# One kernel, one core: turning k and q by DVE blocks and DRAM, and scoring neighbouring tokens by one product sum per pair

## The reference, cut to what matters

```python
q = silu(q_raw)
log_f = logaddexp(log(lb), log1p(-lb) + log_sigmoid(f_raw))   # lb is 0 here: log_sigmoid(f_raw)
k = (1.0 - lb) * sigmoid(-f_raw)
...                                           # per chunk of 64 tokens, 8 heads of 128 channels
G = cumsum(g_t, axis=1)                       # g = log_f
att[t, s] = sum_c q[t, c] * k[s, c] * exp(G[t, c] - G[s, c])    # for s <= t
o_intra = att @ v
```

## Time and profile before

| | |
|---|---|
| time before, 3 runs | 2002.93 us (2002.09 to 2003.38) |
| the profiled execution, its own time | 2004.01 us |
| its span, first to last instruction | 2002.2 us |
| granted TensorE clock, mean | 0.999 |
| PE busy | 1988.7 us, 99% |
| DVE busy | 1723.3 us, 86% |
| ACT busy | 1212.6 us, 61% |
| PE on the chain that ended last | 91% |

### The profile page before, as it was taken

The page is one execution under the profiler, slowest core; times in us unless marked ns, Lnnn a source line. Parts: engine busy times, 40 slices in busy tenths (PEclk is TensorE's granted clock), DMA queues, the critical chain, the costliest instruction groups (busy, mean ns, idle before and its releaser), DMA issues.

```text
span 2002.2 us, 24409 instructions
## 1 busy us (share of the span) xinstructions
PE 1988.7 (99%) x9167; PEld 1647.1 (82%) x9167; DVE 1723.3 (86%) x1641; ACT 1212.6 (61%) x1216; POOL 170.9 (9%) x216
## 2 busy tenths in 40 slices
PE   9999999999999999999999999999999999999998
PEld 7888888888888888888888887888888888888886
DVE  5566776789999999999997467789999999999995
ACT  6755655555666656656657466565656666566664
POOL 0000000100111110111100000100111101111010
PEclk9999999999999999999999999999999999999999
DMA  8764443857898888988877644676988889988886
GB/s 283 253 213 165 157 147 133 280 197 237 267 265 254 248 258 253 268 253 258 246 238 227 194 144 147 218 235 226 268 262 253 248 248 271 262 261 246 252 238 185
DMA packets 237652, 463.50 MB, mean 231 GB/s; under 512 B 16561, under 2 KB 20945, under 8 KB 237457
## 3 DMA queue, kind: packets, MB, share of 16 engines
q1 hardware_dynamic: 203296, 389.08, 57.8%
q0 software_dynamic: 30496, 69.22, 16.5%
q10 hardware_dynamic: 3792, 4.34, 0.7%
HBM read 403.21 MB, written 17.29 MB: 210 GB/s over the span
## 4 chain that ended last, share of the span: by engine, by line
PE 91%; DVE 4%; DMA 2%; ACT 2%; issue 1%; SPq 0%; ACTq 0%; DVEq 0%
PE ps L1823 60%; PE ps L1623 28%; DMA raw<-in_w_ab_in 2%; PE ps L1714 1%; DVE w_lo L969 1%; DVE g_lo L1352 1%; DVE w_lo L1359 0%; PE ps L1981 0%; PE ps L1956 0%; ACT junk L544 0%; ACT w_hi L499 0%; PE ps L1969 0%; DVE w_sum L1340 0%; PE ps L1647 0%; DVE w_sum L1338 0%
## 5 line engine op out<-in xcount | busy, mean ns | idle before, releaser
L1352 DVE TENSOR_TENSOR g_lo<-g_raw,g_hi 128x2048 fp32r<-128x2048 f32 x240 | 545.7, 2287 | 6.5 <-ACT g_hi L768 0.5
L969 DVE TENSOR_TENSOR w_lo<-raw,w_hi 128x1024 fp32r<-128x1024 f32 x247 | 293.1, 1220 | 146.3 <-ACT w_hi L499 145.4
L759 ACT CAST g_hi<-g_raw 128x2048 fp32r<-128x2048 f32 x120 | 229.9, 1916 | 219.5 <-DVE g_raw L1326 215.8
L499 ACT ACTIVATE w_hi<-raw 128x1024 fp32r<-128x1024 f32 x247 | 253.2, 1055 | 146.3 <-DMA raw<-in_w_ab_in 56.5
L1623 PE MATMUL ps<-w_hi,xT_hi 128*128 128x512 f32 x672 | 264.2, 393 | 3.2 <-DVE w_lo L969 2.8
L1823 PE MATMUL ps<-g_hi,xT_hi 128*128 128x512 f32 x680 | 265.4, 390 | 0.1
L1823 PE MATMUL ps<-g_hi,xT_lo 128*128 128x512 f32 x680 | 264.6, 389 | 0.0
L768 ACT CAST g_hi<-g_raw 128x2048 fp32r<-128x2048 f32 x120 | 225.5, 1912 | 60.2 <-PE ps L1823 60.2
L1623 PE MATMUL ps<-w_hi,xT_lo 128*128 128x512 f32 x672 | 261.7, 389 | 0.0
L1623 PE MATMUL ps<-w_lo,xT_hi 128*128 128x512 f32 x672 | 261.5, 389 | 0.0
L1823 PE MATMUL ps<-g_hi,h0T_hi 128*128 128x512 f32 x640 | 249.2, 389 | 0.0
(11 more groups left out here) (232 smaller groups left out, 3134.2 us busy)
## 6 DMA issues: line engine op xcount, KB each, us to landing
g_raw<-in_w_ffn_in SPq DMA_DIRECT2D x320, 512.0 KB, 4.8
g_raw<-in_w_ffn_out SPq DMA_DIRECT2D x160, 512.0 KB, 4.8
raw<-in_w_ab_in SPq DMA_DIRECT2D x95, 512.0 KB, 4.9
x<-y POOLq DMA_DIRECT2D x80, 512.0 KB, 6.9
raw<-in_w_qkv SPq DMA_DIRECT2D x40, 512.0 KB, 4.6
raw<-in_w_ab_out SPq DMA_DIRECT2D x32, 512.0 KB, 4.7
raw<-in_w_ffn_in SPq DMA_DIRECT2D x32, 512.0 KB, 4.9
raw<-in_w_c_out SPq DMA_DIRECT2D x32, 512.0 KB, 5.0
```

Of the source, the lines that this page charges most:

```text
L499: act.activation(w_hi[:, s, :], raw[:, s % RAWS, :], ACT.Copy).then_inc(hi_ready, 1)
L759: act.copy(dst[:, 0:4, :].rearrange("p s w -> p (s w)"), src[:, :, :].rearrange("p s w -> p (s w)")).then_inc(group_hi_ready, 1)
L969: dve.tensor_tensor(w_lo[:, s, :], raw[:, s % RAWS, :], w_hi[:, s, :], ALU.subtract).then_inc(lo_ready, 1)
L1352: ins = dve.tensor_tensor(lo_part[:, 0:4, :].rearrange("p s w -> p (s w)"), src[:, :, :].rearrange("p s w -> p (s w)"), hi_part[:, 0:4, :] ...
```

## The change

PE's 32 transposes of k and q are gone, and so is the level for distance 1.

- k and q are turned like x: DVE turns blocks of 32 x 32 (`turn_kq`, L1162 of the changed kernel), POOL issues one DMA per token tile to DRAM and four back (`kq_dram` to `kq_rows`), and DVE copies the k rows to `kT`, ACT the q rows to `qT`, from SBUF instead of PSUM.
- The scores at distance 1 are one number per pair of tokens (2m, 2m+1) and head. POOL's DMAs gather the odd tokens of `lf` (`f_odd`) and of `q_tok` (`q_odd`) and the even ones of `kk` (`k_even`) into 128 rows. ACT takes the exponential of `f_odd`, DVE multiplies it by `k_even`, then by `q_odd`, sums over channels (`pair_sum`), two small DMAs bring the sums back to token rows, and DVE puts them into the scores through the same mask (`keep_pairs`).
- The other levels stay where they were, one per round from round 6 on.

```diff
+            def carry_out_kq(m):
+                pool.wait_ge(kq_turned, m + 1)
+                pool.dma_start(kq_dram[m % 2], kq_blk[m % 2][:, :, :, :].rearrange("p j h b -> p j (h b)")
+                               ).then_inc(kq_out[m % 2], 16)
+            def carry_in_kq(m):
+                i = m % 2
+                pool.wait_ge(kq_out[i], 16 * (m // 2 + 1))
+                if m >= 2:
+                    pool.wait_ge(kT_copied, i + 1)
+                for j in range(4):
...
+                    pool.dma_start(kq_rows[i][32 * j:32 * (j + 1), :, :, :].rearrange("p i h b -> p i (h b)"),
+                                   src).then_inc(kq_rows_in[i], 16)
...
+            gather(f_odd, lf, 1, f_odd_in)
+            pool.wait_ge(k_ready, 2)
+            gather(k_even, kk, 0, k_even_in)
+            carry_out_kq(0)
+            carry_out_kq(1)
+            carry_in_kq(0)
+            carry_in_kq(1)
+            pool.wait_ge(ab_read, 4)
+            pool.wait_ge(fk_ready, 1)
+            gather(q_odd, q_tok, 1, q_odd_in)
+            carry_out_kq(2)
+            carry_out_kq(3)
+            carry_in_kq(2)
+            carry_in_kq(3)
...
                 if r == 5:
                     ahead(5, 1)
                     for t in range(NT):
-                        act.wait_ge(item_done, 5 + t)
-                        act.copy(qT[:, t, :], side[t]).then_inc(side_free[t], 1)
+                        act.wait_ge(kq_rows_in[t], 128)
+                        act.copy(qT[:, t, :].rearrange("p (h i b) -> p h i b", h=HEADS, i=4),
+                                 kq_rows[t][:, :, :, :].rearrange("p i h b -> p h i b"))
...
+                if r == 3:
+                    act.wait_ge(f_odd_in, 32)
+                    act.activation(f_odd[:, :], f_odd[:, :], ACT.Exp).then_inc(f_odd_ready, 1)
                 if r - 1 == I_R:
+                    act.wait_ge(kq_turned, 2)
+                    act.wait_ge(pair_ready, 1)
...
                 if r == 4:
                     ahead(4, 0)
                     for t in range(NT):
-                        dve.wait_ge(item_done, 3 + t)
-                        dve.tensor_copy(kT[:, t, :], side[t]).then_inc(side_free[t], 1)
+                        dve.wait_ge(kq_rows_in[t], 64)
+                        dve.tensor_copy(kT[:, t, :].rearrange("p (h i b) -> p h i b", h=HEADS, i=4),
+                                        kq_rows[t][:, :, :, :].rearrange("p i h b -> p h i b")).then_inc(kT_copied, 1)
...
-            chunks(3, 0, 3, *X, PAIR[1])
-            for t in range(NT):
-                pe.wait_ge(k_ready, t + 1)
-                turn_tokens(2 + t, kk[:, t, :])
-            chunks(3, 3, 8, *X, PAIR[1])
+            chunks(3, 0, 8, *X, PAIR[1])
             pe.wait_ge(ab_read, 3)
-            chunks(4, 0, 4, *X, PAIR[0])
+            chunks(4, 0, 8, *X, PAIR[0])
             pe.wait_ge(ab_read, 4)
-            for t in range(NT):
-                turn_tokens(4 + t, q_tok[:, t, :])
...
```

More of the change, by code:

```diff
@@ L216, in trunk @@
         fnorm = sb("fnorm", [P, D], at=bias_at + 40 * KB)
+        k_even = sb("k_even", [P, 1024], at=at_mix + 4 * KB)
+        f_odd = sb("f_odd", [P, 1024], at=r1 + 16 * KB)
+        q_odd = sb("q_odd", [P, 1024], at=r1 + 16 * KB)
+        kq_blk = [sb(f"kq{i}_blk", [P, 4, HEADS, 32], at=r1 + (28 + 4 * i) * KB) for i in range(2)]
+        kq_rows = [sb(f"kq{i}_rows", [P, 4, HEADS, 32], at=r1 + (36 + 4 * i) * KB) for i in range(2)]
         x_blk = [sb(f"x{i}_blk", [P, 4, 4, NT, 32], at=r1 + (28 + 4 * i) * KB) for i in range(2)]
@@ L234, in trunk @@
         x_dram = [nc.dram_tensor(f"x{i}_dram", [P, 4, 8 * 32], F32, kind="Internal").ap() for i in range(2)]
+        kq_dram = [nc.dram_tensor(f"kq{i}_dram", [P, 4, 8 * 32], F32, kind="Internal").ap() for i in range(2)]
         ps = ctx.enter_context(nc.psum_tensor("ps", [P, 8, W], F32))
@@ L1112, in _ @@
                     dve.wait_ge(ab_read, 4)
+                    for t in range(NT):
+                        turn_kq(2 + t, q_tok)
                     eye = consts[:, C_IDENT:C_IDENT + 1, :].broadcast_to([P, HEADS, P])
+                    ahead(4, 7)
+                    dve.wait_ge(f_odd_ready, 1)
+                    dve.wait_ge(k_even_in, 32)
+                    dve.tensor_tensor(k_even[:, :], f_odd[:, :], k_even[:, :], ALU.mult).then_inc(fk_ready, 1)
                     for t in range(NT):
[L1115 to L1116 removed]
+                        if t:
+                            ahead(5, 0)
+                        after(dve.tensor_tensor(E[:, 0, :], q_tok[:, t, :], kk[:, t, :], ALU.mult))
+                        after(dve.tensor_reduce(o_sum[:, t, :], E[:, 0, :].rearrange("p (h d) -> p h d", h=HEADS), AX.X, ALU.add))
                         diag = o_sum[:, t, :].rearrange("p (h o) -> p h o", o=1).broadcast_to([P, HEADS, P])
@@ L1119, in _ @@
                     ins.then_inc(att_diag, 1)
+                if r == 3:
+                    dve.wait_ge(rel_out, 16)
+                    for t in range(NT):
+                        dve.wait_ge(k_ready, t + 1)
+                        turn_kq(t, kk)
                 if r == 2:
@@ L1691, in _ @@
             pe.wait_ge(ab_read, 2)
-            chunks(3, 0, 3, *X, PAIR[1])
-            for t in range(NT):
-                pe.wait_ge(k_ready, t + 1)
-                turn_tokens(2 + t, kk[:, t, :])
-            chunks(3, 3, 8, *X, PAIR[1])
+            chunks(3, 0, 8, *X, PAIR[1])
             pe.wait_ge(ab_read, 3)
-            chunks(4, 0, 4, *X, PAIR[0])
+            chunks(4, 0, 8, *X, PAIR[0])
             pe.wait_ge(ab_read, 4)
-            for t in range(NT):
-                turn_tokens(4 + t, q_tok[:, t, :])
[L1702 to L1715, removed]
+            chunks(5, 0, 8, *X, PAIR[1])
+            for r in range(6, 11):
+                pe.wait_ge(ab_read, r - 1)
+                chunks(r, 0, 8, *X, PAIR[r % 2])
+                for t in range(NT):
+                    pe.wait_ge(side_free[t], r - 5)
+                    pe.wait_ge(scaled, 2 * (r - 6) + t + 1)
+                    for h in range(HEADS):
+                        c = slice(h * P, (h + 1) * P)
+                        ins = pe.matmul(side[t][:, c], E[:, t, c], E[:, t, c], start=True, stop=True)
+                    ins.then_inc(item_done, 1)
             pe.wait_ge(ab_read, 10)
```

119 lines of the change are left out of this document (77 added, 42 removed).

## The result

The changed kernel takes 2014.43 us (median of 6 runs, 2013.57 to 2015.9) beside 2002.38 us of the kernel before on the same chip (6 runs, 2001.22 to 2003.38): 1.0057 times as long, 95% interval 1.0047 to 1.0067. It is slower by 12 us, where I had forecast 2002.3 and a range that ended at 2009.5.

A forecast was written before the change was run, and what follows sets the result against it. PE, busy 99% of the span, was taken to bound the kernel. Removing 8.3 us and adding 7.7 us of waits gave -0.6 us, forecast 2002.3 us on the scale of the median; the range ran from just below 1994.6 to 2009.5.

The forecast's parts named there:

- What goes: PE work and waiting removed: wait for G 1.34, turns of k 1.74 and q 1.67, first level 3.57; 8.3 us.
- the two places: New PE waits at (4,1), behind kT's copies, 2.0 us, and at (5,2), behind qT's copies, 5.7 us.
- 7.7 us of waiting in all: PE's total new waiting at (4,1) and (5,2) in the likeliest case, which had chance 0.40.
- The gathers of f_odd and k_even: Gathers starting around 75 us, claimed to cost nothing unless a landing takes over 8 us.
- The round trip of k: k's tiles ready at 87.6 and 88.8 us, 6.5 to first read, second copy to kT ends at 104.8.
- My bound for T, 109.2: Slow case for the second copy to kT, with landings of 8.9 and 8.1 us; PE waits 6.4 us.
- The turn of q: From second copy to kT until the lo of (5,2): 31.5 us, ready at 136.3, where PE wanted 128.6.
- idle DMA engines: During q's trip, DMA share 0.11 assumed: 5.0 us to first read, last landing 4.1 us.
- Rival 3, the clock: PE's granted clock falls during the wait at (5,2); chance 0.12.
- Rival 2, slow issues of POOL: POOL's issues in both turns take 1.02 instead of 0.553 us, 7.5 us more, 2009.8 us; chance 0.20.
- The rival's other condition: Both turns of k and q meeting landings near 8 us, with the same slower end as slow POOL issues.
- Hidden: Exponential of f_odd, 1 us, delays the hi of (3,6) within PE's some 3 us in hand, costing nothing.

The follow-up runs named there:

- experiment 5: Changed kernel with all three gathers and their waits out, the pair product reading other rows: 2003.42 us, ratio 0.9996 to the kernel before.
- experiment 9: Changed kernel with q's ways out ahead of the gather of q_odd on POOL and dynamic_dma_scratch_size 1792: 2007.81 us, ratio 1.0023.
- experiment 2: Changed kernel with q's ways out to DRAM ahead of the gather of q_odd on POOL: 2013.64 us, ratio 1.0050.
- experiment 10: Experiment 1 with the lo of (5,0) and (5,1) ahead of the diagonal's parts and kT's copies behind it: 1999.17 us, ratio 0.9983.
- experiment 1: Changed kernel with kT's copies behind the first pair product on DVE, qT's behind the hi of (5,7) on ACT: 1998.69 us, ratio 0.9977.
- experiment 4: Changed kernel with 24 matmuls nobody reads on PE ahead of (4,1) and 24 ahead of (5,2): 2013.85 us, ratio 1.0059.
- experiment 6: Changed kernel with only the turns of k and q; first level of scores stays on PE, no gathers or pair product: 2007.85 us, ratio 1.0022.
- experiment 11: Only the turns, as experiment 6, but with late copies and the DVE order of experiment 10: 2000.21 us, ratio 0.9985.
- experiment 3: Changed kernel with dynamic_dma_scratch_size 1792 instead of 1024: 2014.31 us over four executions; ratio 1.0056 from three.
- experiment 8: Changed kernel with late copies, lo of (5,0), (5,1) ahead of the diagonal, f/k gathers and pair product later, scratch size 1792: 2001.85 us, ratio 0.9991.
- experiment 7: Changed kernel with only the pair sum on DVE; k and q turned on PE as before: 2007.15 us, ratio 1.0020.

## Why the prediction was wrong

**What goes** was right: 8.3 us of PE and the wait for G, gone from its profile. So were the two places and the mechanism, copies that hold the weights' hi and lo back. The failed step is the size of the term "7.7 us of waiting in all", for which after has 15.5 (1.24, 7.54 and 6.70), and with it the clock, which the sum put at nothing and gave a chance of 0.12.

The table sets the round trips against the rows; T is the end of the second copy to kT, and in the last three columns all is read from the timelines.

| step, us | forecast | after | no gathers | 2 and 3 together |
|---|---|---|---|---|
| k leaves for DRAM, at | 87.6 | 91.56 | 87.46 | 91.99 |
| k: first out to first read | 6.5 | 8.3 | 9.1 | 7.9 |
| k: first read to second copy | 10.0 | 10.8 | 11.6 | 10.4 |
| T, at | 104.8 | 111.3 | 108.9 | 111.0 |
| T to q leaving | 15.2 | 15.3 | 9.0 | 9.4 |
| q: first out to first read | 5.0 | 6.0 | 4.3 | 5.4 |
| q: first read to second copy | 8.0 | 9.8 | 11.0 | 12.2 |

- **The gathers of f_odd and k_even**, put at nothing "unless a landing takes over 8 us", are the first part of what was missing. I asked whether their own result would be in time (f_odd was: it landed in 4.9 us in the median), not what they would do to the loads beside them. The transfers of after from 74 to 92 us, by queue (packets, MB, share of the 16 engines; q0 is POOL's, q1 SP's) and the landing of SP's loads:
```profile
q0 software_dynamic: 320, 1.05, 40.3%
q1 hardware_dynamic: 1131, 2.19, 37.7%
...
raw<-in_w_ab_in SPq DMA_DIRECT2D x6, 512.0 KB, 9.3
```
  In the same stretch of before, SP moves 2.83 MB and its six loads land in 5.3 us. This sets k's departure back from 87.6 to 91.56, and without the gathers it is at 87.46, as forecast. Taking the gathers away brings T forward by only 2.4 of these 4.0 us, since k's trip is then longer.
- **The round trip of k** is the second part: 10.0 us for the reads was near (10.8), the way out took 8.3 instead of 6.5, in all 2.5 us more. Without gathers the trip is even longer, 21.4 us against a forecast of 17.2, so this term was too small by itself: of the 6.5 us by which T was late, 4.1 stay when the gathers are gone. My bound for T, 109.2, was passed too: it took the slowest landings but the early start.
- **The turn of q** is the third: 31.5 us behind T, it took 34.4. The steps up to its departure were right to 0.1 us in sum; the trip itself was 2.8 us longer. I had counted on idle DMA engines, and they were busy 0.84 of the time from 130 to 140 us: 0.53 with POOL's DMAs, nearly all of them the turn's own, and 0.31 with loads of weights. Which of the two cost the 2.8 us is not shown.
- **Rival 3, the clock**, came true with 2.16 us where I had 1.8. The 1.8 was the excess of the 4.73 us that PE's first 13 matmuls take over 13 times 0.227; the granted clock is 1.00 from 1 to 6 us in that trace, so no run shows 1.8 us as the price of a fallen clock. What the runs show in its place is the 2.16 us, behind the fall to 0.50 at (5,2). That the clock fell at (4,1) as well cost nothing more, since (5,2) had to wait for q.
- **Rival 2, slow issues of POOL**, is refuted: 0.55 us each, the issue at 107.76, beside DVE's copy to kT at 107.44, as well. The rival's other condition, both turns at landings near 8 us, came in part: k's two writes took 8.0 and 8.4 us to land, q's 5.7 and 6.2, and no read took over 6.0.
- **Hidden**: the exponential of f_odd did not stay in its 3 us of slack, since the loads had used them up; 1.24 us of waiting at (3,6), which the longer wait at (4,1) would otherwise have held.

The sum: T later by 6.5 (4.0 of it the late start, 2.5 k's trip), q's turn by 2.9, the clock 2.2: 11.6 us of the 12.1 between forecast and time. That is another question than what the gathers cost in all. Against a kernel without gathers (experiment 5, 11.0 us less), they delay T by 2.4 us and q's departure by 6.3 more, and bring on the clock's 2.2. The 6.3 are order: q leaves behind its gather, and that behind the first pair product. This was in my forecast, at its right size; I had not asked whether it had to be so. It paid only together with the larger area, 6.6 us at the milestone in experiment 9: in experiment 2 nearly all of the 5 us went into the stop, which lasted 5.99 us.

What stays open: why the way out of k takes 7.8 to 9.1 us and that of q 3.7 to 6.4 in most runs, whether the order of experiment 10 gains, whether the pair sum gains at all, and how the 4 us of waits that late copies leave divide between late loads and DVE's order. Moving the gathers elsewhere was tried once only, with other edits.

## What to carry over

When an operation goes from PE to a round trip through DRAM, put its consumer where the result is needed (here more than a round later), and not in its engine's list ahead of work that feeds PE: that alone brought the milestone forward by 15.4 us here. Of a DMA called hidden, ask what it does to the loads that share its time, not only when it lands: beside the gathers they took 9.3 us to land, without them 5.9. And test two suspects together as well: order and area gave about one microsecond each apart and 6.6 together.

## What was unexpected of the hardware

- POOL stopped before an issue though the condition written for it was met. With `dynamic_dma_scratch_size` at 1024, the eighth read of a turn went out 0.35 us after the fourth had landed, in both turns of after and of experiments 1, 2, 4, 5, 6, 10 and 11; with 1792 there was no such stop (4.39 and 4.38 us for the eight reads of k in experiments 3 and 9). How the area is counted is not shown. The kernel before has a stop like it, 3.17 us ahead of a read at 510 us.
- The gathers, copies inside SBUF of every second partition with 4 KB a row, took 2.2 times the DMA time per byte of the loads of weights beside them (after, 74 to 92 us: 40.3% for 1.05 MB, 37.7% for 2.19 MB).
- Issuing the eight reads of 128 KB faster did not bring the last one in faster: issued within 4.4 to 5.4 us (experiments 3, 8 and 9) they took 9.8 to 13.9 us from the first issue to the last landing, and 8.8 to 15.9 us where they were issued within 5.6 to 11.1.
- The granted clock was 0.50 behind each wait of 3.86 to 7.93 us of the stage (after, experiments 2, 3, 5, 6, 7 and 9; in experiment 6, with 4.37 us, it fell 0.6 us after work had begun again), and 1.00 behind waits of 3.00 and 2.38 us (experiments 8 and 9). The length of the last wait alone does not tell: it fell behind 2.07 us in experiment 4 at (4,1), with 24 matmuls ahead of that wait, and not behind the same at (5,2); and at 15.7 us of the profiled executions of experiments 3 and 11 it fell behind a wait of 2.05 and of 1.90 us.
